# The forget product in four column groups, ahead of the second query block

## The reference

```
hn = rmsnorm(x, norm_g)
q, k, v, z, f_logit = jnp.split(hn @ w_in, cuts, axis=-1)      # q, k, v, z: 2048 wide; f_logit: 16
log_f = jax.nn.log_sigmoid((f_logit + b_forget).astype(jnp.float32))
cum = jnp.cumsum(log_f, axis=1)
s = q_t . k_s / sqrt(128) + cum[t] - cum[s], causal             # per head
o = softmax(s) @ v * silu(z)
x = x + o @ w_out
```

## Time and profile before

| | |
|---|---|
| median of the runs | 2581.43 us |
| the profiled execution | 2580.91 us |
| its span, first to last instruction | 2579.2 us |
| granted TensorE clock | 0.999 |
| TensorE busy | 2553.5 us, 99% |
| VectorE busy | 1720.6 us, 67% |
| ScalarE busy | 612.3 us, 24% |
| GpSimd busy | 341.5 us, 13% |

### The profile page before, as it was taken

The page is one execution under the profiler, slowest core; times in us unless marked ns, Lnnn a source line. Parts: engine busy times, 40 slices in busy tenths (PEclk is TensorE's granted clock), DMA queues, the critical chain, the costliest instruction groups (busy, mean ns, idle before and its releaser), DMA issues.

```text
span 2579.2 us, 57925 instructions
## 1 busy us (share of the span) xinstructions
PE 2553.5 (99%) x22218; PEld 2458.9 (95%) x22218; DVE 1720.6 (67%) x3630; ACT 612.3 (24%) x1557; POOL 341.5 (13%) x479
## 2 busy tenths in 40 slices
PE   8999999999999999999999999999999999999998
PEld 7888889989999999999999999999999999999997
DVE  7667667565555556788998954655655655777855
ACT  3222221121001112234334320211211012344311
POOL 0111110010001100143443410211220000000000
PEclk9999999999999999999999999999999999999999
DMA  6444433444444444434334435343343444444443
GB/s 255 146 146 138 142 135 130 166 144 168 167 159 149 160 163 164 163 132 163 150 143 163 150 119 197 134 162 132 131 144 151 163 170 172 169 157 164 178 164 114
DMA packets 63764, 400.71 MB, mean 155 GB/s; under 512 B 6816, under 2 KB 13488, under 8 KB 17584
## 3 DMA queue, kind: packets, MB, share of 16 engines
q1 hardware_dynamic: 62992, 397.20, 41.8%
q0 software_dynamic: 672, 2.11, 0.5%
HBM read 397.17 MB, written 2.11 MB: 155 GB/s over the span
## 4 chain that ended last, share of the span: by engine, by line
PE 94%; DVE 3%; issue 2%; ACT 1%; DVEq 0%; DMA 0%; POOL 0%; SPq 0%; ACTq 0%; POOLq 0%
PE psum L607 68%; PE psum L551 12%; PE psum L560 2%; PE psum L1085 1%; PE psum L582 1%; PE psum L778 1%; PE psum L1094 1%; PE psum L690 1%; PE psum L871 1%; PE psum L988 1%; PE psum L842 1%; PE psum L1046 1%; PE psum L683 0%; PE psum L592 0%; PE psum L718 0%
## 5 line engine op out<-in xcount | busy, mean ns | idle before, releaser
L607 PE MATMUL psum<-h,ring 128*128 128x128 f32 x4384 | 524.3, 275 | 1.9 <-DVE near L1797 1.9
L607 PEld LDWEIGHTS psum<-h,ring 128*128 128x128 f32 x4384 | 506.6, 192 | 2.4 <-DVE wide_c L2304 2.0
L607 PE MATMUL psum<-mix,ring 128*128 128x128 f32 x3994 | 477.7, 275 | 0.4
L607 PEld LDWEIGHTS psum<-mix,ring 128*128 128x128 f32 x3994 | 461.4, 192 | 1.4 <-DVE near L1790 1.3
L551 PE MATMUL psum<-h,ring 128*128 128x256 f32 x1504 | 336.1, 381 | 0.0
L551 PEld LDWEIGHTS psum<-h,ring 128*128 128x128 f32 x1504 | 281.7, 190 | 45.7 <-issue 9.4
L1797 DVE TENSOR_TENSOR near<-psum,near 128x128 f32<-128x128 f32 x143 | 41.3, 289 | 344.9 <-PE psum L607 344.9
L607 PE MATMUL psum<-ring,h 128*128 128x128 f32 x1296 | 153.8, 275 | 0.6 <-DVE near L1797 0.6
L607 PEld LDWEIGHTS psum<-ring,h 128*128 128x128 f32 x1296 | 149.1, 192 | 0.7 <-issue 0.7
L1757 DVE TENSOR_TENSOR ring<-ring 128x1024 f32<-128x1024 f32 x112 | 137.9, 1231 | 0.0
L1154 ACT ACTIVATE w<-psum 128x128 f32<-128x128 f32 x75 | 20.8, 277 | 469.8 <-PE psum L607 469.8
(11 more groups left out here) (494 smaller groups left out, 4029.9 us busy)
## 6 DMA issues: line engine op xcount, KB each, us to landing
ring<-w_out SPq DMA_DIRECT2D x80, 1024.0 KB, 5.1
ring<-w_odd SPq DMA_DIRECT2D x64, 1024.0 KB, 4.9
ring<-w_hgrn SPq DMA_DIRECT2D x64, 1024.0 KB, 5.4
ring<-w_even SPq DMA_DIRECT2D x48, 1024.0 KB, 4.8
ring<-w_nsa SPq DMA_DIRECT2D x48, 1024.0 KB, 5.5
ring<-w_rg SPq DMA_DIRECT2D x40, 1024.0 KB, 5.4
ring<-w_cmp_in SPq DMA_DIRECT2D x8, 1024.0 KB, 4.8
ring<-w_rgg SPq DMA_DIRECT2D x10, 512.0 KB, 6.9
```

What stands on the lines that cost most here:

```text
L607: mm = pe.matmul(dst, stationary, moving, start=new and j == 0, stop=new and j == kh - 1, skip_group_check=not new)
```

## The change

The forget product moves behind the first of the two query products and becomes four sums side by side: matmul k writes to partitions 32t to 32t+31 with t = k mod 4, so each group of 32 partitions of bank 6 holds the sum over four of the 16 tiles. Its stationary operand is 32 columns wide (16 weights and 16 zeros), so that all 128 partitions are written; the load grows from 128 to 256 KB. ScalarE copies the four parts, and one matmul with a 0/1 matrix `pick` adds them, behind the second query product. The norm's two matmuls now stand within the first query product.

On VectorE the forms of pair 1 move between the second and the third sum, the first sum and the fourth form of pair 1 come behind the query copies, then the forget steps, and the cumulative sums (`forget_sums`) come behind the three forms of pair 2. ScalarE's exponential and logarithm (`forget_log`) come behind its first copy of pair 1. The constants grow by 16 columns (64 bytes per partition), so buffers allocated after them move by as much.

```diff
-        forget = Phase(1, 1, [Load(7, tiles("w_forget", 0), KT * HEADS, 1)])
+        forget = Phase(1, 0, [Load(7, tiles("w_forget", 0), KT * 2 * HEADS, 7)])
...
+            wait_load(pe, odd1, 0, 0)
+            pe.wait_ge(first_read, after(2 * fast_odd.first))
+            unscaled(lambda k: tile(odd1, 0, k), bank[3][:, 0:T], raw, KT, lambda: norm(0), 4, 6)
             wait_load(pe, forget, 0, 0)
-            unscaled(lambda k: at(7, k * HEADS, (k + 1) * HEADS), bank[6][0:HEADS, 0:T], raw, KT, lambda: norm(0))
+            for k in range(KT):
+                t = k % 4
+                mm = pe.matmul(bank[6][32 * t:32 * t + 32, 0:T], at(7, 2 * k * HEADS, 2 * (k + 1) * HEADS), raw[:, k, :],
+                               start=k < 4, stop=k >= KT - 4)
+                if k >= KT - 4:
+                    mm.then_inc(f_parts, 1)
...
                 if first:
-                    for e in range(2):
-                        wait_load(pe, odd1, 0, e)
-                        for k in range(KT):
-                            mm = pe.matmul(bank[3 + e][:, 0:T], tile(odd1, e, k), raw[:, k, :], start=k == 0,
-                                           stop=k == KT - 1)
-                        mm.then_inc(used, 1 if e else 6)
+                    wait_load(pe, odd1, 0, 1)
+                    pe.wait_ge(later_read, after(5 * fast_odd.first))
+                    for k in range(KT):
+                        mm = pe.matmul(bank[4][:, 0:T], tile(odd1, 1, k), raw[:, k, :], start=k == 0, stop=k == KT - 1)
+                    mm.then_inc(used, 1)
+                    pe.wait_ge(f_kept, after(1))
+                    pe.matmul(bank[6][0:HEADS, T:2 * T], ccol("pick"), wide_a[:, 4, :], start=True, stop=True)\
+                        .then_inc(f_sum, 1)
...
-            s.wait_ge(f_in, after(1))
-            st.mark(s.activation(fl[:, 2, :], fl[:, 1, :], ACT.Exp, scale=-1.0))
-            st.settle()
-            s.activation(fl[:, 3, :], fl[:, 2, :], ACT.Ln, bias=ccol("ones", 0, 1)[0:16, :]).then_inc(f_ln, 1)
+            s.wait_ge(f_parts, after(4))
+            s.activation(wide_a[:, 4, :], bank[6][:, 0:T], ACT.Copy).then_inc(f_kept, 1)
...
-                first_reads(fast_odd, i, 1, k_two)
+                if first:
+                    first_reads(fast_odd, i, 1, k_two, None, forget_log)
+                else:
+                    first_reads(fast_odd, i, 1, k_two)
...
-            sums(sums_odd, h[:, 0:8, :], h[:, 8:16, :], 8)
-
-            v.wait_ge(used, done(forget, 0, 1))
-            then(v.tensor_tensor(fl[:, 0, :], bank[6][0:HEADS, 0:T], rstd[0:HEADS, :], ALU.mult))
...
+            sums(sums_odd, h[:, 0:8, :], h[:, 8:16, :], 8, range(2))
             v.sem_inc(forms_made, 2)
             three_forms(fast_odd, 0, 1)
+            sums(sums_odd, h[:, 0:8, :], h[:, 8:16, :], 8, range(2, 4))
             for e in range(2):
...
+            first_sum(fast_odd, 0, 1)
             fourth_form(fast_odd, 0, 1)
-            v.wait_ge(f_ln, after(1))
...
+            v.wait_ge(f_sum, after(1))
+            then(v.tensor_tensor(fl[:, 0, :], bank[6][0:HEADS, T:2 * T], rstd[0:HEADS, :], ALU.mult))
...
-                three_sums(fast_odd, i, 1, k_two)
+                if not first:
+                    first_sum(fast_odd, i, 1)
+                two_sums(fast_odd, i, 1, k_two)
                 three_forms(fast_odd, i, 2)
+                if first:
+                    forget_sums()
                 fourth_sum(fast_odd, i, 1, k_two)
```

More of the change, by code:

```diff
@@ L76 @@
     ("seen_c", 2 * NCMP), ("slopes", HEADS), ("time", T), ("level", NEAR * TB),
-    ("chunk", T)])
+    ("chunk", T), ("pick", HEADS)])
 class Steps:
@@ L384, in program @@
         g_made = signal("g_made")
+        f_parts, f_kept, f_sum = signal("f_parts"), signal("f_kept"), signal("f_sum")
         pair_mean, final_mean, final_guess = signal("pair_mean"), signal("final_mean"), signal("final_guess")
@@ L576, in norm_pair, with unscaled @@
                     .then_inc(sum_ready, 1)
-            def unscaled(stationary, dst, x_raw, raw_from, between=None, place=4):
+            def unscaled(stationary, dst, x_raw, raw_from, between=None, place=4, units=1):
                 for k in range(KT):
@@ L584, in unscaled @@
                         between()
-                mm.then_inc(used, 1)
+                mm.then_inc(used, units)
             def norm_of_squares():
@@ L1279, in _, with forget_log @@
             norm(1)
-            s.wait_ge(f_in, after(1))
-            st.mark(s.activation(fl[:, 2, :], fl[:, 1, :], ACT.Exp, scale=-1.0))
-            st.settle()
-            s.activation(fl[:, 3, :], fl[:, 2, :], ACT.Ln, bias=ccol("ones", 0, 1)[0:16, :]).then_inc(f_ln, 1)
+            s.wait_ge(f_parts, after(4))
+            s.activation(wide_a[:, 4, :], bank[6][:, 0:T], ACT.Copy).then_inc(f_kept, 1)
+            def forget_log():
+                s.wait_ge(f_in, after(1))
+                st.mark(s.activation(fl[:, 2, :], fl[:, 1, :], ACT.Exp, scale=-1.0))
+                st.settle()
+                s.activation(fl[:, 3, :], fl[:, 2, :], ACT.Ln, bias=ccol("ones", 0, 1)[0:16, :]).then_inc(f_ln, 1)
             def two_heads(i, first):
@@ L2104, in _ @@
             v.wait_ge(h_ready, after(2 * KT))
-            sums(sums_odd, h[:, 0:8, :], h[:, 8:16, :], 8)
-            v.wait_ge(used, done(forget, 0, 1))
-            then(v.tensor_tensor(fl[:, 0, :], bank[6][0:HEADS, 0:T], rstd[0:HEADS, :], ALU.mult))
-            then(v.tensor_scalar(fl[:, 0, :], fl[:, 0, :], pcol("b_forget")[0:16, :], None, ALU.add))
-            v.scalar_tensor_tensor(fl[:, 1, :], fl[:, 0, :], -1.0, fl[:, 0, :], ALU.mult, ALU.max).then_inc(f_in, 1)
+            sums(sums_odd, h[:, 0:8, :], h[:, 8:16, :], 8, range(2))
             v.sem_inc(forms_made, 2)
             three_forms(fast_odd, 0, 1)
+            sums(sums_odd, h[:, 0:8, :], h[:, 8:16, :], 8, range(2, 4))
             for e in range(2):
@@ L2116, in _, with forget_sums @@
                 copied.then_inc(later_read if e else first_read, 5 if e else 2)
+            first_sum(fast_odd, 0, 1)
             fourth_form(fast_odd, 0, 1)
-            v.wait_ge(f_ln, after(1))
[L2119 to L2123, removed]
+            v.wait_ge(f_sum, after(1))
+            then(v.tensor_tensor(fl[:, 0, :], bank[6][0:HEADS, T:2 * T], rstd[0:HEADS, :], ALU.mult))
+            then(v.tensor_scalar(fl[:, 0, :], fl[:, 0, :], pcol("b_forget")[0:16, :], None, ALU.add))
+            v.scalar_tensor_tensor(fl[:, 1, :], fl[:, 0, :], -1.0, fl[:, 0, :], ALU.mult, ALU.max).then_inc(f_in, 1)
+            def forget_sums():
+                v.wait_ge(f_ln, after(1))
+                then(v.tensor_scalar(fl[:, 1, :], fl[:, 0, :], 0.0, None, ALU.min))
+                then(v.tensor_tensor(fl[:, 2, :], fl[:, 3, :], fl[:, 1, :], ALU.subtract))
+                then(v.tensor_scalar(fl[:, 2, :], fl[:, 2, :], P ** 0.5, None, ALU.mult))
+                v.tensor_tensor_scan(nc_[:, :], ccol("ones", 0, 1)[0:16, :].to_broadcast([16, T]), fl[:, 2, :], 0.0,
+                                     ALU.mult, ALU.add).then_inc(cum_made, 1)
             def two_heads(i, first, last):
@@ L2683, in shape_constants @@
     put("eps", EPS)
+    put("pick", np.tile(np.eye(2 * HEADS)[:, 0:HEADS], (4, 1)))
     return c
@@ L2763, in lay_out @@
         w_out1=blocks(i["w_out_even"][0]),
-        w_forget=cut(wo, 8192, HEADS)[None, None],
+        w_forget=np.pad(cut(wo, 8192, HEADS).reshape(P, KT, HEADS), ((0, 0), (0, 0), (0, HEADS)))
+        .reshape(1, 1, P, -1),
         w_odd1=series(wo, [[D * m + P * (n + TWO_HEADS * e) for m in range(4) for e in range(2)]
```

## The result

The changed kernel takes 2587.1 us (median of 18 runs, 2582.99 to 2588.57), the kernel before, on the same chip, 2581.59 us (18 runs, 2580.55 to 2584.4). The medians are 5.5 us apart; the ratio of the means is 1.0017, with a 95% interval of 1.0010 to 1.0023: slower, by about 0.2%. The profiled execution of after took 2587.76 us (span 2586.1), of before 2580.91 (span 2579.2): 6.9 us of span to explain.

A forecast was written before the change was run, and what follows sets the result against it. TensorE was taken to bound the kernel: -4.65 saved, +1.75 wait at pair one, +1.6 at pair three gave -1.3 us from 2580.91, so 2579.6 profiled, 2580.1 as a median; range 2577.0 to 2583.2.

The forecast's parts named there:

- The grouped product: TensorE's forget product in four column groups: four rounds in 1.86 us instead of 7.11.
- Rival 3: Forget product: the groups run one after another, so the kernel is slower by 2.1 us, 2583.5; chance 4%.
- The sum on TensorE: TensorE's own time from the stretch's start to pair one: 17.4 us instead of 22.09, saving 4.65.
- The wait at pair one: TensorE waits 1.75 us for VectorE's first query copy before pair one, leaving a gain of 2.9 us.
- The cumulative sums: VectorE's sums, now behind pair two's three forms, end at 552.7, 6.8 us later than before.
- The chain of GpSimd: From the sums through write and broadcast to GpSimd's masks: ready at 563.4, 0.8 us over the quiet case.
- the quiet case: GpSimd's chain without added DMA delay: 9.9 us from the sums, masks at 562.6 at the earliest.
- The prediction's own sign: Stated test at GpSimd's masks: the prediction is wrong if they end after 564.7.
- rival 2: Pair three: late masks, write behind loads (2582.5 to 2584.7 us), plus GpSimd issues held by VectorE (up to 2.4); 15%.
- The wait in pair three: TensorE waits 1.5 us for VectorE before product 2 of pair three, beginning at 569.1 instead of 567.6.

The follow-up runs named there:

- e8: e5 with pair one no longer waiting for the first query copy; both copies count in what product 2 waits for; 2578.03 us.
- e1: The changed kernel with the forget steps right behind the query copies and the cumulative sums ahead of pair one's sums; 2578.72 us.
- e2: The changed kernel with SyncE holding the first of the two loads until the small write of the cumulative sums has landed; 2586.99 us.
- e4: The changed kernel's column groups with VectorE and ScalarE in the order of before, parts added ahead of the second query product; 2581.6 us.
- e5: e1 with the last of the four sums moved behind the two query copies; 2579.38 us.
- e6: e4 with five matmuls, results not used, filling TensorE's pause ahead of pair one; 2580.93 us.
- e3: The changed kernel with nine matmuls, results not used, in TensorE's pause ahead of product 2 of pair three; 2583.44 us.
- e7: e1 without the column groups: forget product as one sum of 16 columns, no copy of parts, no summing matmul; 2581.24 us.
- e9: e8 with four matmuls, results not used, in TensorE's pause at about 1100 us; 2576.89 us.
- e10: The kernel before with four matmuls, results not used, in TensorE's pause at about 1100 us; 2581.78 us.

## Why the prediction was wrong

Its forecast was -1.3 us in the profiled execution; the place gave +3.65. Step by step:

- **The grouped product**, 1.00 + 2 x 0.43 = 1.86 us: measured 1.86. The Trainium skill, "TensorE: Matmul & The Clock Gate", measured speedup against the span model, gives 3.07 times for four row tiles and 2.38 times for three column tiles, and no figure for four column groups; here it was 7.11 / 1.86 = 3.8 times, so the measurement decides. Rival 3 (the groups don't overlap) fell.
- **The sum on TensorE**, 17.4 us: e8, without a wait, shows 17.37.
- **The wait at pair one**, 1.75 us: measured 1.77. The saving there, forecast 2.9, was 2.88.
- **The cumulative sums**, forecast 552.7: their end in after is 554.26, less the 1.54 by which its whole stretch is later 552.72.
- **The chain of GpSimd** is the first of the two steps that failed: "I take 0.8 more than the quiet case, 563.4, because most of the loads' data has passed by 555.6". 552.7 to 563.4 is 10.7 us; from 554.26 to the masks' end at 568.15 it took 13.9. Over the quiet chain that is 4.0 us in place of 0.8. The loads' data had passed when the broadcast left at 561.13, but not when the write left, 1.1 us behind the second load: the sum took both loads as begun at 550.4, though the earlier trace rows has 2.11 us for two of them (552.01 and 553.80 in after), and two loads issued then, landing 5.9 us later in the median, are not mostly past by 555.6. I had taken a dearer landing of the write (6.2, in the earlier trace rows that of a broadcast) into the range and not into the sum. It landed in 5.9, 4.0 over the quiet 1.9. The prediction's own sign came: the masks end after 564.7, at 568.15 or, less the 1.54, at 566.6. This is rival 2's mechanism, given 15% and priced 2582.5 to 2584.7. Its other half, GpSimd's issues held by VectorE, did not show: the issue took 0.70 us, as in the earlier trace rows.
- **The wait in pair three**: TensorE could begin product 2 at 569.1 by forecast; 573.98 - 1.54 = 572.4 was measured, 3.3 later. VectorE's steps from masks to fourth sum were right: 5.5 us forecast (563.4 to 568.9), 5.7 measured (568.15 to 573.83).
- **Half clock behind the pause**, 1.7 us, is the second: it stood in no term, nor in rival 2's price. The profile of before has a pause of 1.86 us with full clock behind it, and I took idle time to cost only itself. -1.3 + 3.3 + 1.7 = 3.7, which is the +3.65. The Trainium skill, "TensorE: Matmul & The Clock Gate", HAM oscillation, describes matmuls that begin at half rate behind a wait; the trace agrees (0.51 behind the 4.60 us pause). I had not asked it of a pause that I forecast myself.

What stays open: why the same pause is followed by half clock in one kernel and not in another (1.77 and 1.78 us at pair one of after and e1: no; 1.77 in e2: yes; 1.85 or 1.86 us near 1100: yes in after, e2, e4, e5, e6 and e8, no in before, e1, e3 and e7), and what part of the medians' distance, 5.5 against the 3.65 of the place, is the drop near 1107, which after's profile has and before's has not. That the half clock comes of the idle time was tried by filling the pause at three places (e3, e6, e9, and in before e10); each filled place was at 1.00. These are single profiles, and unfilled pauses of 1.8 us were at 1.00 in some as well, so it is best shown for the pause of 4.60 us, where the runs of e3 agree, and likely for the shorter ones.

## What to carry to other kernels

When a change moves a chain that ends in a DMA, lay its two ends over the issue times of the big loads and price each DMA apart: here a 16 KB write 1.1 us behind a 1 MB load cost 4 us, and holding the loads back only handed the cost to the next copy. A new pause of TensorE has to be priced with what the clock may do behind it, here 1.7 us behind pauses of 1.8 to 4.6 us, in some runs and not in others. And a faster piece of TensorE is worth only what the next engine leaves of it: of 4.7 us saved 2.9 arrived, until the copy that held pair one was no longer waited for (e8).

## What the runs showed of the hardware

- A 16 KB write from GpSimd's queue lands in 1.9 us in quiet (before, e1, e2) and in 5.9 beside two 1 MB loads (after); the 256 KB broadcast takes 8.3 us beside them (e2), and GpSimd waits 7.4 (e1) and 7.7 us (e2) for it in place of 4.3. The 6.2 us of the earlier trace rows was no upper bound.
- Within the span, behind its first 15 us, the half clock came in pieces of 3.4 us each time, at 0.50 or 0.51, ten pieces in the twelve profiles, and always behind a pause of TensorE of 1.8 to 4.6 us; each cost 1.6 to 1.7 us. One such piece is as large as what the groups brought alone (e4: 1.73 us of stretch), so a profile has to be searched for them before two kernels are compared.
- Matmuls whose results are not used cost nothing in a pause where TensorE waits anyway (e6: a stretch of 20.35 us against 20.36 without them), and the clock was at 1.00 behind them in e3, e6, e9 and e10.
